# The conv feed-forward's up projection as 512-column matmuls in two PSUM banks, and wide runs of both banks put together in all feed-forward loops

## What is computed

```python
# first block, once per layer (conv0, conv1)
up = depthwise_conv(h @ ffn_w_up[l], ffn_conv_w[l], ffn_conv_b[l])       # width 3, over the tokens
f = (jax.nn.silu(up[..., :D_FF]) * up[..., D_FF:]) @ ffn_w_down[l]
h = layer_norm(DEEPNORM_ALPHA * h + f, ln_ffn_g[l], ln_ffn_b[l])

# second block, twice per layer (ffn1.0, ffn2.0, ffn1.1, ffn2.1)
gate, up = jnp.split(h @ wi, 2, axis=-1)
x = x + 0.5 * (jax.nn.silu(gate) * up) @ wo
```

## Time and profile before

| | us |
|---|---|
| median of 3 runs | 1793.12 (1792.72 to 1794.09) |
| the profiled execution, own time | 1794.38 |
| its span in the trace | 1792.6 |
| PE busy in it | 1761.7 (98%) |
| DVE busy | 1319.7 (74%) |
| ACT busy | 958.9 (53%) |

### The profile page before, as it was taken

The page is one execution under the profiler, slowest core; times in us unless marked ns, Lnnn a source line. Parts: engine busy times, 40 slices in busy tenths (PEclk is TensorE's granted clock), DMA queues, the critical chain, the costliest instruction groups (busy, mean ns, idle before and its releaser), DMA issues.

```text
span 1792.6 us, 28818 instructions
## 1 busy us (share of the span) xinstructions
PE 1761.7 (98%) x10644; PEld 1547.7 (86%) x10657; DVE 1319.7 (74%) x1782; ACT 958.9 (53%) x1293; POOL 98.4 (5%) x90
## 2 busy tenths in 40 slices
PE   8999999999999999999999999999999999999999
PEld 7978998896898988888998988888888886888887
DVE  6999877799987787666787656666666677557666
ACT  5556555547555555445546555444644467655443
POOL 1001100000300000000170000000000000000000
PEclk9999999999999999999999999999999999999999
DMA  9626755553574637555534635555555541525553
GB/s 333 181 99 197 253 190 179 164 157 117 183 263 168 210 124 258 189 185 164 178 110 164 240 114 183 192 187 187 187 192 186 197 142 50 186 95 194 187 197 125
DMA packets 236626, 318.51 MB, mean 178 GB/s; under 512 B 14342, under 2 KB 206758, under 8 KB 236038
## 3 DMA queue, kind: packets, MB, share of 16 engines
q1 hardware_dynamic: 230838, 295.44, 49.6%
q0 software_dynamic: 5424, 20.35, 3.5%
q10 hardware_dynamic: 288, 1.69, 0.2%
HBM read 313.27 MB, written 4.19 MB: 177 GB/s over the span
## 4 chain that ended last, share of the span: by engine, by line
PE 88%; DVE 7%; ACT 2%; issue 2%; DMA 1%; SPq 1%; DVEq 0%; ACTq 0%
PE bank L1070 20%; PE bank L1055 20%; PE bank L744 16%; PE bank L1073 10%; PE bank L946 7%; PE bank L767 2%; DVE w_lo L2402 2%; PE bank L753 1%; PE bank L772 1%; PE bank L831 1%; PE bank L1230 1%; DVE work L2399 1%; ACT w_hi L1738 1%; PE bank L1152 1%; SPq L3603 1%
## 5 line engine op out<-in xcount | busy, mean ns | idle before, releaser
L2402 DVE TENSOR_TENSOR w_lo<-raw,w_hi 128x2048 fp32r<-128x2048 f32 (+2 forms) x283 | 639.6, 2265 | 208.9 <-ACT w_hi L1738 205.9
L1738 ACT ACTIVATE w_hi<-raw 128x2048 fp32r<-128x2048 f32 (+2 forms) x278 | 527.5, 1900 | 292.3 <-PE bank L1070 156.0
L1070 PE MATMUL bank<-xt_both,w_hi 128*128 128x512 f32 x1600 | 400.3, 392 | 0.0
L1070 PEld LDWEIGHTS bank<-xt_both,w_hi 128*128 128x128 f32 x1600 | 291.6, 189 | 54.6
L744 PE MATMUL bank<-xt_both,w_hi 128*128 128x256 f32 (+1 forms) x1840 | 334.7, 284 | 0.2
L744 PEld LDWEIGHTS bank<-xt_both,w_hi 128*128 128x128 f32 (+1 forms) x1840 | 285.3, 190 | 2.5 <-issue 1.6
L1738 ACT ACTIVATE work<-bank 128x256 f32<-128x256 f32 (+3 forms) x290 | 120.8, 427 | 283.3 <-PE bank L1073 256.9
L744 PE MATMUL bank<-xt_both,w_lo 128*128 128x256 f32 (+2 forms) x920 | 260.1, 283 | 0.0
L1073 PEld LDWEIGHTS bank<-xt_both,w_lo 128*128 128x128 f32 x1600 | 218.3, 190 | 15.6
L1073 PE MATMUL bank<-xt_both,w_lo 128*128 128x256 f32 x1600 | 223.1, 282 | 0.0
L1055 PE MATMUL bank<-w_hi,act_hi 128*128 128x512 f32 x528 | 206.7, 392 | 0.2
(11 more groups left out here) (362 smaller groups left out, 1960.8 us busy)
## 6 DMA issues: line engine op xcount, KB each, us to landing
raw<-in_ffn_wi SPq DMA_DIRECT2D x88, 1024.0 KB, 5.1
raw<-in_ffn_w_up SPq DMA_DIRECT2D x44, 1024.0 KB, 5.1
raw<-in_ffn_wo SPq DMA_DIRECT2D x44, 1024.0 KB, 4.9
raw<-in_ffn_w_down SPq DMA_DIRECT2D x22, 1024.0 KB, 5.3
raw<-in_ssd_in_proj SPq DMA_DIRECT2D x14, 1024.0 KB, 5.4
raw<-in_w_in SPq DMA_DIRECT2D x8, 1024.0 KB, 7.1
raw<-in_w_out SPq DMA_DIRECT2D x8, 1024.0 KB, 4.9
raw<-in_even_out_proj SPq DMA_DIRECT2D x8, 1024.0 KB, 4.8
```

What stands on the lines that cost most here:

```text
L1070: first(mm(bank[b][:, :], w[0][:, k, P * j:P * j + P], xt_both[:, k, :, :].rearrange("p v t -> p (v t)"), start=k == 0, stop=False))
L1738: return act.activation(dst, src, ACT.Copy)
L2402: return dve.tensor_tensor(out=out, in0=in0, in1=in1, op=op)
```

## The change

1. `pair_halves` takes the place of `tile_halves`, in all six loops: 8 wide matmuls into the first bank, 8 wide into the second, then 8 narrow into the first and 8 narrow into the second. The second bank's `bank_drained` is waited for after the first wide run.
2. In the two conv loops the up unit goes the same way, into banks 2 and 3 in every chunk: 16 matmuls of 512 columns and 16 of 256 in the place of 48 of 256.
3. ACT copies the up banks' halves too, and DVE adds them, into the same `f_sum` that the gate's sums used; `center` and `taps` of up then read `f_sum` and no longer PSUM.
4. ACT's silu of the gate stands ahead of the up copies, and the high split of unit 3c+3 behind the up center.

```diff
-                def tile_halves(b, w, j, first):
...
+                def pair_halves(banks, w, first, freed):
+
+                    for j, b in enumerate(banks):
+                        freed(b)
+                        for k in range(KT):
+                            first(mm(bank[b][:, :], w[0][:, k, P * j:P * j + P],
+                                     xt_both[:, k, :, :].rearrange("p v t -> p (v t)"), start=k == 0, stop=False))
+                    for j, b in enumerate(banks):
+                        for k in range(KT):
+                            ins = mm(bank[b][:, 0:T], w[1][:, k, P * j:P * j + P], xt_hi[:, k, :], start=False,
+                                     stop=k == KT - 1)
+                        ins.then_inc(bank_full[b], 1)
...
+                gate_banks, up_banks = ((1, 3), (0, 2)) if scaled else ((1, 0), (2, 3))
...
-                            pe.wait_ge(bank_drained[2 + c % 2], base[2 + c % 2] + i)
-                            up_pair(k + 1, 2 + c % 2, i)
+                        for banks, kk in ((gate_banks, k), (up_banks, k + 1)):
+                            w, first = split_unit(kk, i, KT), First()
+                            pair_halves(banks, w, first,
+                                        lambda b: pe.wait_ge(bank_drained[b], i * 2 + base[b] + c - 1))
...
                         center(c, f_sum, f_gate, 0, i)
-                        b, n = names.of[f"{tag}.u{c}"]
-                        act.wait_ge(bank_full[b], i + n)
-                        center(c, halves(b), f_up, 22, i)
-                        split_in_loop(tag, 3 * c + 3, i)
                         act.wait_ge(gate_tapped, seen.next(gate_tapped))
                         silu(c)
+                        copy_halves("u", c, i)
+                        act.wait_ge(halves_summed, seen.next(halves_summed, 2))
+                        center(c, f_sum, f_up, 22, i)
+                        split_in_loop(tag, 3 * c + 3, i)
...
                         taps(c, f_sum, f_gate, 0, i).then_inc(gate_tapped, 1)
-                        b, n = names.of[f"{tag}.u{c}"]
-                        taps(c, two(bank[b][:, :]), f_up, 22, i).then_inc(bank_drained[b], 1)
-                        dve.wait_ge(bank_drained[b], i + n)
+                        sums("u", c, i)
+                        step(taps(c, f_sum, f_up, 22, i))
                         product(c)
```

More of the change, by code:

```diff
@@ L1094, in ffn_any @@
                         down(k + 2, c - 1, i)
                 for c in (1, 2):
-                    for banks, what in (((1, 3), "g"), ((0, 2), "u")):
-                        if scaled:
-                            for j, b in enumerate(banks):
-                                names.of[f"{tag}.{what}{c}.{j}"] = (b, base[b] + c)
-                                names.fills[b] = base[b] + 2 * TURNS
-                        else:
-                            if what == "g":
-                                for j, b in enumerate((1, 0)):
-                                    names.of[f"{tag}.g{c}.{j}"] = (b, base[b] + c)
-                                    names.fills[b] = base[b] + 2 * TURNS
-                            else:
-                                b = 2 + c % 2
-                                names.of[f"{tag}.u{c}"] = (b, base[b] + 1)
-                                names.fills[b] = base[b] + TURNS
+                    for banks, what in ((gate_banks, "g"), (up_banks, "u")):
+                        for j, b in enumerate(banks):
+                            names.of[f"{tag}.{what}{c}.{j}"] = (b, base[b] + c)
+                            names.fills[b] = base[b] + 2 * TURNS
@@ L1950, in halves, with copy_halves @@
                     return bank[b][:, :].rearrange("p (a b) -> p a b", a=2)
-                def copy_halves(c, turn):
+                def copy_halves(what, c, turn):
                     for j in range(2):
-                        b, n = names.of[f"{tag}.g{c}.{j}"]
+                        b, n = names.of[f"{tag}.{what}{c}.{j}"]
                         act.wait_ge(bank_full[b], turn * 2 + n)
-                        copy(f_low[:, 0, j, :], bank[b][:, T:2 * T]).then_inc(half_copied, 1)
+                        copy(f_low[:, "gu".index(what), j, :], bank[b][:, T:2 * T]).then_inc(half_copied, 1)
                 def silu(c):
@@ L2789, in taps, with sums @@
                     return ins
-                def sums(c, turn):
+                def sums(what, c, turn):
                     for j in range(2):
-                        b, n = names.of[f"{tag}.g{c}.{j}"]
+                        b, n = names.of[f"{tag}.{what}{c}.{j}"]
                         dve.wait_ge(half_copied, seen.next(half_copied))
-                        tt_(f_sum[:, j, :], bank[b][:, 0:T], f_low[:, 0, j, :], ALU.add).then_inc(bank_drained[b], 1)
+                        tt_(f_sum[:, j, :], bank[b][:, 0:T], f_low[:, "gu".index(what), j, :],
+                            ALU.add).then_inc(bank_drained[b], 1)
                     for j in range(2):
-                        b, n = names.of[f"{tag}.g{c}.{j}"]
+                        b, n = names.of[f"{tag}.{what}{c}.{j}"]
                         dve.wait_ge(bank_drained[b], turn * 2 + n)
```

28 lines of the change are left out of this document (5 added, 23 removed).

## The result

The changed kernel takes 1800.88 us, the median of 7 runs (1798.08 to 1804.14); the kernel before takes 1794.09 beside it, the median of 7 (1791.71 to 1795.09). The ratio is 1.0042, with a 95% interval of 1.0033 to 1.0051: **6.8 us slower**. The forecast of 1804.7 had the sign and, the clock apart, the mechanism; it was 4 us too high.

What follows compares the result with a forecast made beforehand. PE was taken as the bound, with conv DVE level at two places. Per conv loop 4.3 + 0.8 + 1.6 = 6.7; twice, 13.4, less 1.8 scaled: 11.6 slower than 1793.12, 1804.7 us, range 1797 to 1811.

Steps and rivals of the forecast that it cites:

- the clock: After the two new 3.1 us PE waits per conv loop: each drop costs 1.6 us, 0.8 of it reaching DVE's chain at up(2).
- PE's gain: Conv chunks on PE: 0.20 us less in up, 0.02 in gate, 0.22 per chunk; 6.2 us together with the scaled loops.
- The scaled loops: Four loops of ten chunks: wide runs following wide ones save 0.045 us per chunk, 1.8 us in all (bounds 1.2 to 2.4).
- the relay: DVE to ACT and back between gate's last tap and up's first: silu, copies, second add, center and handshakes, 3.20 us.
- the start: Chunk 2 of conv loops: low split of unit 6 starts at 200.43, so PE waits 3.1 us before up(2).
- The early wait for bank 0: Chunk 1: holds gate(1) up by some 0.7 us, but free, since down(0) waits for DVE's split anyway.
- the loop and the end: DVE-ACT cycle of 16.48 us level with PE's 16.57; last down 4.3 us later per conv loop, after a 3.1 us wait.
- the short wait at up(3): PE waits 0.2 us at up(3) in the conv loops, because that unit's low split is that much late.
- rival 2: DVE and ACT bound every chunk: handshakes 0.3 more make the cycle 16.8, 1.9 us more per conv loop, 1808.5; chance 0.18.
- Rival 1: The clock stays up through the new conv-loop waits: 6.8 us slower, 1799.9; chance 0.20.
- rival 3: Relay near 2.4 us, cycle 15.7, DVE catches up in four chunks: about 2.3 per conv loop, +3 us, 1796; chance 0.10.
- rival 4: Only PE counts, DVE's idle time takes the whole relay: PE's 6.2 us gained, 1786.9; chance 0.06.

Runs made afterwards that it cites:

- e2: Changed kernel with wide up unit, but no up copies or sums, up's taps reading PSUM directly, low-part pass never added: 1787.35 us, ratio 0.9964 to the kernel before.
- e6: e3 with the last turn's second conv chunk doing its up unit as before (48 narrow matmuls, one bank, no sums): 1789.02 us, ratio 0.9972 to the kernel before.
- e8: e6 with gate's blocks in turn again in the conv loops (wide and narrow of block 0, then of block 1): 1788.68 us, against 1788.61 for e9.
- e4: Changed kernel with one more unused ACT activation between silu and up's copies, making the relay 0.54 us longer: 1813.23 us, ratio 1.0109 to the kernel before.
- e7: The changed kernel run once more, unchanged, on another occasion: 1800.39 us against 1794.08 for the kernel before, ratio 1.0034.
- e3: Changed kernel reordered: up copies and high split ahead of silu, low split between up's sums and taps, own up sum buffer: 1796.2 us, ratio 1.0016 to the kernel before.
- e5: Changed kernel with ten 512-column matmuls of zeros on TensorE before the last down of both conv loops: 1800.81 us, against 1800.39 for the changed kernel.
- e9: The kernel of e6 run once more, beside e8: 1788.61 us, ratio 0.9967 to the kernel before.

## Why the prediction was right or wrong, point by point

**Right: PE's gain.** 0.22 a chunk gives a period of 16.57: measured 16.57 (gate's taps start at 243.83 and 260.40), and with the sums away the whole gain arrives (e2). The scaled loops were put at -1.8: measured -1.9. Wide matmuls at 0.228 us against two narrow ones at 0.24 carried the first term, and the second was the 0.02 us by which a wide run is shorter behind a wide one. The estimate by the column formula of the Trainium skill (TensorE: Matmul & The Clock Gate, section "Wait — 56ns, not 53.3ns?"), 0.8 us in the place of 4.0, is not borne out by e2, which gained 5.7 to 6.2 in all, about 1.8 of it in the scaled loops. By the earlier trace rows the steps are longer than that formula's by 12 ns at 512 columns and by 10 to 11 at 256, not by 12 to 13 at both; the argument does not change.

**Right: the relay.** Put together from six rows as 3.20 us: measured 3.19. Its parts were 0.03, 0.63, 0.64, 0.42, 0.24, 1.09 and a guess of 0.15; the handshakes measured 0.03, 0.23 and 0.14. That the sum fits to 0.01 is partly luck: the copies start 0.09 before silu ends (194.16 against 194.25), and the second add ends 0.52 behind the copies (195.32 against 194.80), not 0.42. With every handshake at 0.24 the sum is 3.5, not the 3.6 of the prediction.

**Right: the start.** The low split of unit 6 was to start 23.73 us behind gate(1) (200.43 - 176.70): measured 200.61 - 176.90 = 23.71. The wait of PE was put at 3.1 and is 2.85 to 2.89, since PE itself is later: the wait for bank 0.

**The early wait for bank 0** was called free because down(0) waits for DVE's split anyway. It does hold gate(1) up by 0.7: the second wide run starts 2.67 behind the first (176.90 to 179.57), where the first run took 2.02 (176.70 to 178.72) before; 0.48 is the part in which PE is seen idle. But down(0) comes 0.3 later. The split that was to hide this reaches only 0.26 beyond PE (before, down(0) came 11.79 behind gate(1), and PE's own work was 11.53: 5.77 for gate, 5.76 for up). In the changed kernel the 0.3 is off the path all the same, since DVE decides at up(2), so the sum did not suffer. Where DVE doesn't decide, down(0) itself is late: in e6 by 0.3 in each loop. Taking the wait away gave nothing back at the last down, though (e8).

**Mostly right: the loop and the end.** The last down was to come at 349.2 to 349.9, and I took 349.6, 4.3 later than before. Conv1, with a full clock, has 3.9, which is the lower end (349.2 - 176.70 = 172.5; measured 172.51). Part of that match is luck. The second product came 38.43 behind gate(1) (523.55 - 485.12) where 38.7 was forecast, since the split of unit 7 followed that of unit 6 at once and did not have to wait. The eight periods from it to the tenth product (655.70) average 16.52, between the 16.48 and the 16.57 of the forecast; the first is 16.51. These are the two products on DVE:

```profile
523.55 0.69 DVE L2387 TENSOR_TENSOR work<-work 128x512 f32<-128x512 f32 x1
...
655.70 0.69 DVE L2387 TENSOR_TENSOR work<-work 128x512 f32<-128x512 f32 x1
```

The wait at the last down was put at 3.1 and is 2.5; the short wait at up(3) that I added isn't there. 0.4 too much per loop, 0.8 in all. e4 shows how close the two periods are: some 0.5 us more in the relay makes the cycle 17.0 and costs what rival 2 describes, and more.

**Wrong: the clock.** The step was "each costs between 0 and 1.7; I take 1.6", with 0.8 of it reaching the chain at up(2): 2.4 per loop, 4.8 in all. The size of one drop was right, and at up(2) too low: in e7's trace conv0 has one drop there and takes 173.97 from gate(1) to the last down, conv1 none and takes 172.50, so 1.5 of the 1.7 arrive. What failed is "three of three waits over 2 us dropped it" as a reason for "always": those three were one execution, the 6.7 us before its first matmul left aside, and in e2's the clock fell behind one of the same three. Behind the four new waits of the changed kernel's two profiled executions the clock fell 3 times in 8, and over many runs its mean granted clock is 0.9973 against 0.9977 of the kernel before; at 1.4 us for each 0.001 that is some 0.6 us of the 4.8 (0.2 to 0.7 by what the medians leave). Rival 1, where the clock stays up, gave 6.8, the first measured difference, but by two errors that cancel: its loops are 0.4 too long each, and the clock did fall in some runs.

The sum again: 2 x 3.9 - 1.8 + (0.2 to 0.7) = 6.2 to 6.7, against 6.3 and 6.8 measured. (0.2 to 0.7 is the remainder of those two, so only the 6.0 is a check.) The forecast of 11.6 slower was 4.8 above the first difference, 6.8: about 4 were the clock and 0.8 the end. The time itself was missed by 3.8, since the kernel before came out 1.0 higher than the 1793.12 that the forecast started from.

**Rivals 3 and 4** fell with the relay's 3.19 us. (In rival 3 DVE would have caught up in three chunks, 2.3 at 0.9 each, not four; its sum does not use the four.) e3 and e6 show what rival 4 would have needed: DVE work placed in the relay, and no relay in the last chunk.

## What to carry to other kernels

When a matmul saves time by leaving a sum to the engines that evict it, count the longest chain from the last matmul to the next thing TensorE needs, engine by engine, and not the busy shares: DVE was 74% busy here, and 3.2 us of relay cost 3.9 us a loop. Put work that is independent into the relay's gaps, and see how the loop's last turn ends, where nothing follows that could cover it: the two together, the split moved into the relay and the last chunk done in the old way, turned 6 us of loss into 5 of gain (e6), where the first alone was 2.7 slower than before, 0.3 at the same clock (e3). For a clock that falls behind waits, compare runs with the same mean granted clock first, and then ask how often it fell.

## What the runs showed of the hardware that I had not expected

Whether the granted clock falls behind a wait of TensorE was not certain where the wait was under 3 us. Counted in the eleven profiled executions of this study, without the waits of the program's first 10 us:

| wait of PE, us | place | clock 0.50 behind it |
|---|---|---|
| 3.4 | up(2) and last down, e4 | 4 of 4 |
| 3.0 | last down, e3 | 2 of 2 |
| 2.8 to 2.9 | up(2), changed kernel twice, e5 | 3 of 6 |
| 2.5 | last down, changed kernel twice | 1 of 4 |
| 1.9 to 2.2 | near 46 us, e4, e6, e9 | 2 of 3 |
| 2.0 | near 55 us, all but e4 and e9 | 8 of 9 |
| 2.1 | near 123 us, all eleven | 10 of 11 |
| 2.1 | near 420 to 435 us, all eleven, the same code | 4 of 11 |

The last two rows are one wait of one length at two places, so its length alone does not decide; what differs between them is not settled here. The Trainium skill, TensorE: Matmul & The Clock Gate, section "What's actually happening", has the chip's watch over activity run freely, not started anew with a kernel, and calls the number of slow matmuls at a kernel's start variable from run to run for that reason. The scatter here agrees with that, but no run here separates it from other causes. Each drop took away the same: summed over the stretch where the clock was 0.50, 1.7 us of full clock, and once two followed each other (203 to 209 in the changed kernel, 3.4 us).
